# Gathering the tokens of two experts with one plain fp32 matmul in place of a pair of split fp32r ones

## The reference

```python
def moe_swiglu(x, w_router, b_router, we_gate, we_up, we_down):
    logits = (x @ w_router).astype(jnp.float32) + b_router.astype(jnp.float32)
    top_v, top_i = lax.top_k(logits, TOP_K)
    top_w = jax.nn.softmax(top_v, axis=-1)
    gates = jnp.sum(jax.nn.one_hot(top_i, N_EXPERTS, dtype=jnp.float32) * top_w[..., None], axis=-2)
    out = jnp.zeros(x.shape, jnp.float32)
    for e in range(N_EXPERTS):
        out = out + gates[..., e:e + 1] * swiglu(x, we_gate[e], we_up[e], we_down[e]).astype(jnp.float32)
    return out.astype(x.dtype)
```

## Time and profile before

| | us |
|---|---|
| time, median of 3 runs | 1092.96 (1087.98 to 1094.05) |
| the profiled execution's own time | 1092.77 |
| its span | 1090.9 |
| TensorE matmul busy | 983.4 (90%) |
| VectorE busy | 715.6 (66%) |
| ScalarE busy | 493.3 (45%) |
| mean granted TensorE clock | 0.931 of full |

### The profile page before, as it was taken

The page is one execution under the profiler, slowest core; times in us unless marked ns, Lnnn a source line. Parts: engine busy times, 40 slices in busy tenths (PEclk is TensorE's granted clock), DMA queues, the critical chain, the costliest instruction groups (busy, mean ns, idle before and its releaser), DMA issues.

```text
span 1090.9 us, 15207 instructions
## 1 busy us (share of the span) xinstructions
PE 983.4 (90%) x5594; PEld 819.2 (75%) x5594; DVE 715.6 (66%) x1052; ACT 493.3 (45%) x622; POOL 329.9 (30%) x271
## 2 busy tenths in 40 slices
PE   4997978899999997988795699999999999999995
PEld 2575756899999995465574588887888788878773
DVE  3679862635243418499626638698969796988873
ACT  3350041544334412610304237677767766776752
POOL 4995000311111108990002003313331423142320
PEclk8997789899999998995997579999999999999997
DMA  9200180554654209000630048889888988898961
GB/s 291 103 1 3 42 319 12 167 157 157 175 157 154 69 4 323 9 1 3 251 143 1 1 137 318 288 298 377 270 291 299 370 271 294 302 370 274 371 204 44
DMA packets 71512, 199.65 MB, mean 183 GB/s; under 512 B 9664, under 2 KB 31328, under 8 KB 71328
## 3 DMA queue, kind: packets, MB, share of 16 engines
q1 hardware_dynamic: 69408, 192.89, 51.9%
q0 software_dynamic: 2048, 6.01, 1.8%
HBM read 197.27 MB, written 1.61 MB: 182 GB/s over the span
## 4 chain that ended last, share of the span: by engine, by line
PE 66%; DVE 23%; ACT 5%; DMA 3%; issue 2%; DVEq 0%; SPq 0%; ACTq 0%
PE ps L1095 7%; PE ps L1094 7%; PE ps L1097 7%; PE ps L882 6%; PE ps L881 6%; PE ps L883 6%; PE ps L1008 6%; DVE U L1213 5%; DVE M L1213 4%; PE ps L1165 4%; DVE D L1213 4%; PE ps L1084 4%; PE ps L1166 3%; PE ps L1169 3%; PE ps L876 2%; ACT D L732 2%
## 5 line engine op out<-in xcount | busy, mean ns | idle before, releaser
L689 ACT ACTIVATE wrnd_g<-wraw_g 128x1376 fp32r<-128x1376 f32 (+2 forms) x96 | 115.4, 1214 | 64.8 <-DMA wraw_g<-in_moe_w_down 32.2
L565 POOL TENSOR_TENSOR wrnd_g<-wraw_g,wrnd_g 128x1024 fp32r<-128x1024 f32 (+2 forms) x16 | 47.0, 2941 | 321.1 <-ACT wrnd_g L689 321.1
L1213 DVE TENSOR_TENSOR wrnd_g<-wraw_g,wrnd_g 128x1376 fp32r<-128x1376 f32 (+1 forms) x80 | 123.0, 1550 | 21.4 <-ACT wrnd_g L689 21.3
L1213 DVE TENSOR_TENSOR wrnd_u<-wraw_u,wrnd_u 128x1376 fp32r<-128x1376 f32 (+1 forms) x80 | 131.5, 1676 | 3.4 <-ACT wrnd_u L689 2.9
L689 ACT ACTIVATE wrnd_u<-wraw_u 128x1376 fp32r<-128x1376 f32 (+1 forms) x96 | 115.6, 1256 | 11.1 <-DMA wraw_u<-in_moe_w_gate 6.7
L1213 DVE TENSOR_TENSOR xb<-xb,ps 128x288 f32<-128x288 f32 x96 | 39.5, 449 | 73.8 <-PE ps L1008 49.2
L565 POOL TENSOR_TENSOR wrnd_u<-wraw_u,wrnd_u 128x1376 fp32r<-128x1376 f32 (+1 forms) x16 | 55.5, 3467 | 82.1 <-ACT wrnd_u L689 82.1
L1008 PE MATMUL ps<-hb,D 128*128 128x288 f32 x256 | 67.8, 429 | 8.9 <-DVE hb L1438 8.8
L881 PE MATMUL ps<-Md,split_u 128*128 128x288 f32 (+2 forms) x240 | 70.6, 294 | 0.0
L1008 PEld LDWEIGHTS ps<-hb,D 128*128 128x128 f32 x256 | 51.4, 202 | 25.3 <-DVE hb L1438 10.6
L883 PE MATMUL ps<-Md,split_u 128*128 128x288 f32 (+2 forms) x240 | 70.3, 293 | 0.0
(11 more groups left out here) (289 smaller groups left out, 2666.2 us busy)
## 6 DMA issues: line engine op xcount, KB each, us to landing
wraw_u<-in_moe_w_gate SPq DMA_DIRECT2D x39, 688.0 KB, 6.4
wraw_g<-in_moe_w_up SPq DMA_DIRECT2D x32, 688.0 KB, 7.1
wraw_g<-in_moe_w_down SPq DMA_DIRECT2D x39, 512.0 KB, 4.6
wraw_u<-in_moe_w_down SPq DMA_DIRECT2D x33, 512.0 KB, 4.5
wraw_u<-in_moe_w_up SPq DMA_DIRECT2D x24, 688.0 KB, 5.7
wraw_g<-in_moe_w_gate SPq DMA_DIRECT2D x18, 688.0 KB, 5.8
raw<-in_ffn_w_gate SPq DMA_DIRECT2D x20, 512.0 KB, 4.2
raw<-in_ffn_w_up SPq DMA_DIRECT2D x20, 512.0 KB, 3.8
```

Of the source, the lines that this page charges most:

```text
L565: pool.tensor_tensor(lo[0:r, 0:w], raw_half(n)[0:r, 0:w], hi[0:r, 0:w].bitcast(F32), ALU.subtract).then_inc(w_lo_pool, 1)
L689: act.activation(halves(n)[0][0:r, 0:w], raw_half(n)[0:r, 0:w], ACT.Copy).then_inc(w_hi, 1)
L1213: return dve.tensor_tensor(o, a, b, op)
```

## The change

The tokens are copied out of PSUM once, unsplit, as `tok` in plain fp32. The six subtractions on VectorE and their semaphores go. The one-hots `oh` are written as plain fp32. Both lie in `M`, a plain fp32 tensor, at the same columns as in `Me`. Each pair of fp32r matmuls in `gather` becomes one plain fp32 matmul: 24 in place of 48 for each gather. Gathered tokens are rounded and split behind the gather as before.

```diff
-        tok_h = Me[:, 0:3072].rearrange("p (t f) -> p t f", t=3)
-        tok_l = Me[:, 3072:6144].rearrange("p (t f) -> p t f", t=3)
+        tok = M[:, 0:3072].rearrange("p (t f) -> p t f", t=3)
...
-        oh = Me[:, 8960:9728].rearrange("p (t s) -> p t s", t=3)
+        oh = M[:, 8960:9728].rearrange("p (t s) -> p t s", t=3)
...
-                act.activation(tok_h[0:TILES[t][1], t, (n % 2) * 512:(n % 2 + 1) * 512],
-                               ps[0:TILES[t][1], n + 1, :], ACT.Copy).then_inc(tokh_ready, 1)
+                act.activation(tok[0:TILES[t][1], t, (n % 2) * 512:(n % 2 + 1) * 512],
+                               ps[0:TILES[t][1], n + 1, :], ACT.Copy).then_inc(tok_ready, 1)
...
-            pe.wait_ge(tokl_ready, 6)
+            pe.wait_ge(tok_ready, 6)
...
                     for t in (1, 2, 0):
                         n = TILES[t][1]
-                        for z, part in enumerate((tok_h, tok_l)):
-                            mm = pe.matmul(bank(b, 2 * P, (k % 2) * 2 * P), part[0:n, t, k * P:(k + 1) * P],
-                                           oh[0:n, t, :], start=(t == 1 and z == 0), stop=(t == 0 and z == 1))
+                        mm = pe.matmul(bank(b, 2 * P, (k % 2) * 2 * P), tok[0:n, t, k * P:(k + 1) * P],
+                                       oh[0:n, t, :], start=(t == 1), stop=(t == 0))
...
-            for n in range(6):
-                t, f = n // 2, slice((n % 2) * 512, (n % 2 + 1) * 512)
-                w = TILES[t][1]
-                dve.wait_ge(tokh_ready, n + 1)
-                tt(tok_l[0:w, t, f], ps[0:w, n + 1, :], tok_h[0:w, t, f].bitcast(F32),
-                   ALU.subtract).then_inc(tokl_ready, 1)
```

More of the change, by code:

```diff
@@ L391, in build @@
         htok_mm = sem("htok_mm")
-        tokh_ready = sem("tokh_ready")
-        tokl_ready = sem("tokl_ready")
+        tok_ready = sem("tok_ready")
         d_ready = sem("d_ready")
```

## The result

The changed kernel takes 1116.12 us, median of 4 runs (1114.46 to 1118.56); the kernel before takes 1091.6 us in the same comparison. The ratio is 1.0229, 95% interval 1.0191 to 1.0267: 2.3% slower. The profiled execution takes 1117.24 us, 24.5 us more than the profiled one of before. The forecast was 1117.0 us.

A forecast was written before the change was run, and what follows sets the result against it. TensorE was taken to bound the kernel (matmuls busy 90%, 66% of the chain), with all four gathers on the path. From 1092.77 us, -0.3 + 14.3 + 10.2 = +24.2 gave 1117.0 us, range 1112 to 1122.

The forecast's parts named there:

- The subtractions: Ahead of the first gather: removing VectorE's six, 3.67 us long, saves only 0.3 us, bounds 0 and 0.43.
- The distance of two records: Gather matmuls at full clock, 256 columns: 0.217 us between plain fp32 records, 0.118 between fp32r ones, 0.099 more each.
- The r that follows: One r of a loop gather, 12 records: 3.26 us instead of 2.07, bounds 2.60 (row-count changes entirely hidden) and 3.58.
- the three gathers: Gathers in the loop, 144 records at 0.099 us more each: +14.3 us, bounds +6.4 and +18.1.
- The one-hots and the copies: ScalarE's copies and the one-hots: number and size unchanged, cost nothing; at most 1.26 us gained in the first gather.
- The changes of row count: In each gather, four changes between 128-row and 32-row tiles per r, 0.16 us each, the same before and after.
- The first gather: Gather ahead of the gate matmuls: 48 records at 0.213 us more each, +10.2 us, about 25 us long.
- the clock would stay: In the first gather: TensorE's clock stays at half until the gate matmuls; the forecast with this had chance 0.62.
- Rival 1: The clock rises within the first gather, which then takes 15.7 us; total time 1104.7 us; chance 0.25.
- Rival 2: The loop's gathers are partly hidden: 11.1 us of scatter waits shrink by 7.4 us; total 1109.6 us; chance 0.05.
- Rivals 3 and 4: Gathers: plain matmul costs as two fp32r, 1092.5 us, chance 0.04; same with clock rising in first gather, 1084.8, chance 0.02.
- The gate matmuls behind the first gather: Directly behind the first gather: they run at a clock of 0.50 for some 6 us.

## Why the prediction was right

- **The subtractions** were priced at 0.3 us with bounds of 0 and 0.43. The kernel without them shows 0.29 in its timeline, and no difference that can be measured in its time. In the changed kernel the reduction came 0.76 us sooner behind the choice of experts, which is over the 0.43 that the prediction named as a sign of being wrong; but 0.47 of it are position matmuls that ran in part at a higher clock, and 0.29 the subtractions. The step that found this was to look, beside the chain, for the other condition of the instruction behind them.
- **The distance of two records** was 0.217 and 0.118 us by scaling rows of 288 columns; the padded kernels measure 0.215 and 0.119. The r that follows was forecast at 3.26 us and is 3.27; the three gathers +14.3, by the trace +14.4. The padded kernels also bear out the reason given for 3.26 against the bound of 2.60: a change costs 0.19 us behind a plain matmul as behind a split one.
- **The one-hots and the copies**, priced at nothing, cost the same: the six one-hots take 1.25 us before and after, and a copy 0.60 us at the median in both.
- **The changes of row count** were rightly kept in the sum as something that neither grows nor shrinks. Their size was low: 0.16 us, and 0.19 measured. The row used for it ended at the start of the next matmul's record, and behind a change that record starts some 0.1 us early, together with its weight load (it lasts 0.50 us there and 0.39 elsewhere). This was the same before and after, so it fell out of the sum.
- **The first gather**: 25.2 us forecast, 25.20 measured, at a clock of 0.50 to the end. The 0.213 us for each record were a choice between 0.198 and 0.22, and the second of these used 0.22 for a split record at half clock, for which no row is given. (25.20 - 14.96)/48 is 0.213; that it agrees so closely is in part luck. That the clock would stay was the weakest step, with 0.62 for it, argued from a likeness with two stretches in their row counts. Padding the tile takes away the changes and the records of 32 rows together, and the clock rises after 4.0 us: so the argument pointed at the right feature, the row counts, but how they keep the clock down is not shown. Rival 1 was not far: with half the changes the clock does rise within the gather. That kernel is at 1097.43, also because it pays for fewer changes.
- **Rival 2** (part hidden at the scatter) fell: the waits there are 10.2 us in the changed kernel, 11.0 with plain fp32 in the loop alone and 10.1 with plain fp32 in the first gather alone. **Rivals 3 and 4** fell with the 0.215 against 0.119. By the Trainium skill's "FP8 and Floating Point Precision" (TensorE Precision Notes) true fp32 takes four passes. The trace agrees with that, and not with the halved peak of the Trainium skill's "Perfetto Trace Analysis" (Engine Utilization), if that is read as the rate of a plain fp32 matmul: two records of 0.215 us for 256 columns make 0.43 us, which is four times 256 columns at 2.4 GHz and 3.6 times the 0.119 of one fp32r matmul.
- The gate matmuls behind the first gather ran at half clock for 4.5 us where some 6 were forecast, and for 2.8 us in the kernel without subtractions and 5.9 in the one with plain fp32 in the loop alone. At half the speed this is a difference of 1.5 us in the time.
- The chances by outcome (faster 0.03, slower 0.93) are each 0.01 off what the list of rivals adds up to (0.02 and 0.94).

## What to carry to other kernels

Before trading several fp32r matmuls for fewer plain fp32 ones, count records and columns: one plain matmul of 256 columns costs here as much as 3.6 fp32r ones. So it replaces a sum of two products at a loss, as measured, and by the same figures one of three products at a smaller loss, which no run tested. Where the chain shows work that ends only just last, its removal is worth the margin to what ends next, here 0.3 of 3.7 us by the timeline. Keep the number of rows the same from one matmul to the next: zero rows added to a small tile cost nothing on TensorE, and here took 1.7% off the kernel before, to 1073.18 us, the fastest version of this study.

## What the runs showed of the hardware

A change between 128 and 32 active rows costs TensorE 0.19 us at full clock. There the next weight load starts 0.21 us behind the start of the last matmul, where between matmuls with the same rows it starts together with one. At half clock the split gather with eight changes fewer takes 12.76 us against 14.96, some 0.3 us each. The unexpected part is what goes with these row counts: a gather with sixteen stretches of 128 and 32 rows ran for 15 us split, and for 25 us plain, without TensorE's clock leaving 1.2 GHz, though its matmul records leave no pause. With all records at 128 rows the clock was at 2.4 GHz 3.7 to 4.0 us after the start; with half the changes after 7.4 us in plain fp32, and not within 12.8 us split. What in the row counts decides it stays open.
